# Seven block products in two more places and at half depth: a fused two-block network, 512 tokens, one core

## The reference

```python
# first block
mix = sigmoid(g_a) * (fox @ w_fox_up) + sigmoid(g_b) * (nsa @ w_nsa_up)
x = x + mix @ w_out                       # then the expert layer
# second block
proj = rmsnorm(h, g_pre) @ w_in           # gate_logits are its last 2 x 1024 columns
y_a = rwkv7_branch(...)                   # recurrence in chunks of 32 tokens, then @ w_out_a (512 x 1024)
y_b = mla_branch(...)                     # attention, then @ w_out_b (512 x 1024)
g_a, g_b = sigmoid(gate_logits + b_gate)
h = h + rmsnorm((g_a * y_a + g_b * y_b) @ w_o, g_post)
```

## Time and profile before

| | us |
|---|---|
| three runs | 1466.65, 1468.12, 1472.21 |
| median | 1468.12 |
| profiled execution, its time | 1459.77 |
| its span, first to last instruction | 1458.5 |
| PE busy | 1386.6 |
| DVE, ACT, POOL busy | 551.8, 347.0, 272.2 |

### The profile page before, as it was taken

The page is one execution under the profiler, slowest core; times in us unless marked ns, Lnnn a source line. Parts: engine busy times, 40 slices in busy tenths (PEclk is TensorE's granted clock), DMA queues, the critical chain, the costliest instruction groups (busy, mean ns, idle before and its releaser), DMA issues. The chain is left out here.

```text
span 1458.5 us, 24128 instructions
## 1 busy us (share of the span) xinstructions
PE 1386.6 (95%) x10276; PEld 786.6 (54%) x10276; DVE 551.8 (38%) x1338; ACT 347.0 (24%) x827; POOL 272.2 (19%) x311
## 2 busy tenths in 40 slices
PE   7998999899999997999999999999999899999997
PEld 4545544667858445444444434456877445556543
DVE  3124423574111625512211133444359581333403
ACT  2124324543101001111111123444221201322221
POOL 3010302203311641022222122010231002111000
PEclk9899999999999998999999999999999999999999
DMA  6154013220131267799999991010140421300211
GB/s 205 58 200 182 1 58 89 81 96 4 59 115 58 71 246 292 265 372 363 371 380 379 388 340 65 21 58 2 57 173 29 116 87 38 124 3 17 101 73 58
DMA packets 98975, 207.79 MB, mean 142 GB/s; under 512 B 14534, under 2 KB 22545, under 8 KB 98737
## 3 DMA queue, kind: packets, MB, share of 16 engines
q1 hardware_dynamic: 87152, 171.38, 32.7%
q0 software_dynamic: 11712, 34.83, 7.1%
HBM read 185.73 MB, written 19.42 MB: 141 GB/s over the span
## 5 line engine op out<-in xcount | busy, mean ns | idle before, releaser
L471 PE MATMUL pb<-Wt,HT 128*128 128x512 f32 (+1 forms) x384 | 154.7, 562 | 0.5 <-DMA Wt<-in_w_in_dram 0.5
L3620 PE MATMUL pb<-Wt,HT 128*128 128x512 f32 x256 | 117.8, 602 | 2.3 <-DVE AR L3711 2.3
L471 PEld LDWEIGHTS pb<-Wt,HT 128*128 128x128 f32 x384 | 71.4, 207 | 71.0 <-issue 71.0
L2183 PE MATMUL pb<-AR 128*64 128x512 f32 x256 | 85.0, 595 | 0.7 <-issue 0.7
L3620 PEld LDWEIGHTS pb<-Wt,HT 128*128 128x128 f32 x256 | 46.4, 190 | 54.1 <-issue 49.2
L683 PE MATMUL pb<-AR 64*128 64x512 f32 (+7 forms) x256 | 63.6, 494 | 11.1 <-ACT AR L778 4.5
L2183 PE MATMUL pb<-Wt,AR 128*64 128x512 f32 x192 | 70.8, 595 | 0.0
L782 ACT ACTIVATE AR<-AR,SM 128x512 f32<-128x512 f32 (+3 forms) x96 | 53.1, 554 | 51.6 <-DVE SM L734 51.2
L734 DVE CUSTOM_DVE_ANT_0 AR<-pb,AR 128x512 f32<-128x512 f32 (+3 forms) x96 | 43.2, 488 | 57.6 <-PE pb L685 57.4
L1547 PE MATMUL pb<-HT,Wt 128*128 128x256 f32 x288 | 65.0, 380 | 0.0
L3632 PE MATMUL pb<-Wt,AR 128*128 128x512 f32 x128 | 59.9, 605 | 0.9 <-ACT AR L810 0.8
(11 more groups left out here) (569 smaller groups left out, 2411.3 us busy)
## 6 DMA issues: line engine op xcount, KB each, us to landing
Wt<-in_w_in_dram SPq DMA_DIRECT2D x18, 2048.0 KB, 8.1
AR<-in_w_gate_dram SPq DMA_DIRECT2D x8, 2048.0 KB, 18.7
AR<-in_w_up_dram SPq DMA_DIRECT2D x8, 2048.0 KB, 18.7
AR<-in_w_down_dram SPq DMA_DIRECT2D x8, 2048.0 KB, 17.8
Wt<-in_w_gate_dram SPq DMA_DIRECT2D x6, 2048.0 KB, 18.2
Wt<-in_w_down_dram SPq DMA_DIRECT2D x6, 2048.0 KB, 14.2
Wt<-in_w_up_dram SPq DMA_DIRECT2D x6, 2048.0 KB, 21.1
ys<-AR POOLq DMA_DIRECT2D x1, 6144.0 KB, 22.5
```

Source lines behind the costliest of these rows:

```text
L471: r = mm(s[:, 0:n], lT[:, k, t * 128:(t + 1) * 128], w[:, k, c0:c0 + n], start=k == 0, stop=k == nk - 1)
L2183: r = mm(s[o:o + 64, :], XT[b % 2][:, k, 0:64], W.ap((n, b))[:, k, :], start=k == 0, stop=k == 7)
L3620: r = mm(s, HT[:, k, t * 128:(t + 1) * 128], W.ap(("gate2", c, br))[:, k, :], start=k == 0, stop=k == 7)
```

## The change

1. *First merge.* The up projections become `Quarters` units too, of half the depth (`self.h` is 2 instead of 4, so a product has 8 instructions of 256 columns). The order is gate, gate, up, up for each branch; a unit's product 4 comes behind the next unit's product 1. VectorE multiplies the results into the gates as they come and, in the last unit, mixes rows 0 to 3 between. GpSimd gets the left sums of both attention outputs.
2. *Output projection of the first block.* The first right sum moves into the last merge unit, the other sums alternate with the left ones, and the additions of product 1 into X are split: two early, four at the end.
3. *Branch b's gate* becomes two more `Quarters` units (u, v) with channels as rows, bias and sigmoid on ScalarE with a bias column (a new small load at the start), in 28 dense steps; its up projections follow with channels as rows, in 16 steps. Their right sums go behind those of z_a on GpSimd, the group norm's and bias loads and the decayed keys come behind them. The values' turns use rings T and O.
4. *Mixed rows of branch a* are turned tile by tile, at the start of the next tile's gates, and added out of PSUM by VectorE.
5. *Last projection* by `Seven` (`fin7`): 56 instead of 64 matmul pairs, both halves of w_o at its start, GpSimd's sums beside it, and a new order of the last rows.
6. All of GpSimd's sums of blocks are cut into pieces of 512 elements (`tiles_po`).
7. SP loads both gates' weights ahead of both up weights.

```diff
+        def tiles_po(out, a, b, op, sem):
+            n, w = out.shape[1], out.shape[2]
+            s = max(1, 512 // w)
+            for k in range(0, n, s):
+                r = gt.tensor_tensor(out[:, k:k + s, :], a[:, k:k + s, :], b[:, k:k + s, :], op)
+            r.then_inc(sem, 1)
...
+            def right_po(self, between=None):
                 t1, t2, t4 = self.rights
                 b = self.before
-                po.wait_ge(*W.loaded(self.tag))
+                po.wait_ge(*W.loaded(self.name))
                 if b is not None:
                     po.wait_ge(*b.part(1))
-                gt.tensor_tensor(t1, self.b12, self.b11, ALU.subtract).then_inc(self.right_sem, 1)
+                tiles_po(t1, self.b12, self.b11, ALU.subtract, self.right_sem)
                 if b is not None:
                     po.wait_ge(*b.part(2))
                 po.wait_ge(*self.right(1))
-                gt.tensor_tensor(t2, self.b22, t1, ALU.subtract).then_inc(self.right_sem, 1)
-                gt.tensor_tensor(self.b12, self.b22, self.b12, ALU.subtract).then_inc(self.right_sem, 1)
+                tiles_po(t2, self.b22, t1, ALU.subtract, self.right_sem)
+                tiles_po(self.b12, self.b22, self.b12, ALU.subtract, self.right_sem)
...
             def product(self, bank, s, t, go_on=False):
                 for i in range(2):
                     o, q = bank[:, 256 * i:256 * i + 256], slice(128 * i, 128 * i + 128)
-                    for k in range(4):
+                    for k in range(self.h):
                         lhs, rhs = (s[:, k, q], t[:, k, :]) if self.by_rows else (t[:, k, q], s[:, k, :])
-                        m = mm(o, lhs, rhs, start=i == k == 0 and not go_on, stop=k == 3, skip_group_check=True)
+                        m = mm(o, lhs, rhs, start=i == k == 0 and not go_on, stop=k == self.h - 1, skip_group_check=True)
...
+        merge7 = []
         for b, to in enumerate((mix, sg1)):
-            for c in range(2):
-                gates7.append(Quarters(("gate", c, b), 2 * b + c, merge_use, to[:, 4 * c:4 * c + 4, :], False,
-                                       gates7[-1] if gates7 else None))
+            for kind, use in (("gate", gate_use), ("up", up_use[b])):
+                for c in range(2):
+                    tag = ("gate", c, b) if kind == "gate" else ("up", b, c)
...
+            for n, u in enumerate(merge7):
+                u.right_po((lambda: out7.right_po(1)) if n == 7 else None)
+                if n == 0:
+                    left_sums_po(foT, 2, up_sums, s_uleft[0])
+                if n == 4:
+                    po.wait_ge(*P.filled(merge7[3].key("y")))
...
+            for n, u in enumerate(merge7):
+                if n == 2:
+                    pe.wait_ge(s_loc, 1)
+                u.p1_pe()
+                if n:
+                    merge7[n - 1].p4_pe()
+                u.p5_pe()
+                u.p2_pe()
+                u.p6_pe()
+                u.p3_pe()
+                u.p7_pe()
+            u.p4_pe()
 
...
+                    last = b == c == 1
+                    u.p5_ve()
+                    ve.wait_ge(*P.drained(g.key("x")))
+                    ve.wait_ge(*P.filled(u.key("x")))
+                    vt.tensor_tensor(u.c11, u.view("x"), u.c11, ALU.mult).then_inc(P.free(u.key("x")), 1)
+                    u.p6_ve()
+                    if last:
+                        mix_ve(0)
+                    ve.wait_ge(s_sg, 3 * (2 * b + c + 1))
...
         def ffn_norm_po():
-            out7.right_po()
             po.wait_ge(s_mix, 8)
-            out7.left_po(mixT)
+            out7.left_po(mixT, 1)
+            out7.right_po(2)
+            out7.left_po(mixT, 2)
             for i in range(2):
                 po.wait_ge(*out7.first(i))
-                for s in (X[:, i, 512:1024], X[:, 2 + i, 512:1024], X[:, 2 + i, 0:512]):
-                    gt.tensor_tensor(s, s, firsts[i], ALU.add).then_inc(s_fadd, 1)
+                gt.tensor_tensor(X[:, 2 + i, 512:1024], X[:, 2 + i, 512:1024], firsts[i], ALU.add).then_inc(s_fadd, 1)
+            out7.left_po(mixT, 3)
+            out7.right_po(3)
+            out7.left_po(mixT, 4)
+            for t, c in ((0, 512), (1, 512), (2, 0), (3, 0)):
+                gt.tensor_tensor(X[:, t, c:c + 512], X[:, t, c:c + 512], firsts[t % 2], ALU.add).then_inc(s_fadd, 1)
...
+        mx = Place(AR, ARN, tail_at).take(8, 512)
+        gate_use = dict(feature_use, rights=weight_sums[0:2] + [Place(flat_dif, 1024).take(4, 256)])
+        gates_b = []
+        for c in range(2):
+            gates_b.append(Quarters(("gate2", c, 1), len(merge7) + len(units), gate_use, mx[:, 4 * c:4 * c + 4, :], False,
+                                    units[-1]))
+            units.append(gates_b[c])
+        def dif_free_po():
...
-                s = P.take(pe, "S", ("vt", n))
+                s = P.take(pe, "TTOO"[n], ("vt", n))
...
+        def gates_b_pe():
+            u, v = gates_b
+            for f in (u.p1_pe, u.p5_pe, u.p2_pe, u.p6_pe, u.p3_pe, u.p7_pe, v.p1_pe, u.p4_pe, v.p5_pe, v.p2_pe, v.p6_pe,
+                      v.p3_pe, v.p7_pe, v.p4_pe):
+                f()
+                yield 1
+                yield 1
+        def ups_b_pe():
+            pe.wait_ge(s_ob, 4)
+            for m in range(8):
+                c, q = m // 4, slice(128 * (m % 4), 128 * (m % 4) + 128)
+                pe.wait_ge(*W.loaded(("up2", c, 1)))
+                s = P.take(pe, "O", ("ub", m))
+                for k in range(4):
+                    r = mm(s, W.ap(("up2", c, 1))[:, k, q], oBT[:, k, :], start=k == 0, stop=k == 3)
...
+        def mixed_turn_pe(c, t, ring):
+            pe.wait_ge(*P.drained(("u2", 0, c, t)))
+            turn4_pe(("mxt", c, t), sgr[c], 4, ring)
+        def mixed_add_ve(c, t):
+            key, o = ("mxt", c, t), mx[:, 4 * c:4 * c + 4, t * 128:(t + 1) * 128]
+            ve.wait_ge(*P.filled(key))
+            vt.tensor_tensor(o, P.ap(key).rearrange("p (m q) -> p m q", q=128), o, ALU.add).then_inc(P.free(key), 1)
...
+            yield from gates_b_pe()
+            yield from ups_b_pe()
+            for t in ALLT:
+                if t > 0:
+                    mixed_turn_pe(0, t - 1, "O")
                 for c in range(2):
-                    yield from gate_pe(0, c, t)
+                    for i, _ in enumerate(gate_pe(c, t)):
+                        if t > 0 and c == i == 0:
+                            mixed_turn_pe(1, t - 1, "O")
+                        yield 1
                 while t not in ended:
                     yield 1
-                if t == 3:
-                    for u in range(3):
-                        for c in range(2):
-                            mixed_turn_pe(c, u)
-                        yield 1
                 pe.wait_ge(s_out2, t + 1)
                 turn4_pe(("oAt", t), oA[:, t, :], 4, "O")
...
+                if n == 2:
+                    u.p5_ve()
+                if n == 4:
+                    u.p6_ve()
+                if n == 5:
+                    u.c12_ve()
+                if n == 6:
+                    u.c22_ve()
+                if n == 8:
+                    u.c21_ve()
+                if n == 9:
+                    v.p5_ve()
+                if n == 11:
+                    v.p6_ve()
+                if n == 12:
+                    v.c12_ve()
+                if n == 13:
+                    v.c22_ve()
+                if n == 14:
+                    v.c21_ve()
+                if n > 14:
+                    up(n - 15)
...
+            w = fin7.steps_pe(mxT, ready)
+            next(w)
+            for d in range(2):
+                mixed_turn_pe(d, 3, "T")
+            for _ in w:
+                pass
...
+            first_rows(0)
+            with_third(0)
+            first_rows(1)
+            with_third(1)
+            high_gain(0)
+            high_gain(1)
+            with_last(0)
+            low_gain(0)
+            root(2)
+            with_last(1)
+            last_rows(0)
+            low_gain(1)
+            root(3)
+            last_rows(1)
...
-            po.wait_ge(s_yc, 8)
             gt.dma_start(X[:, :, :], xv).then_inc(s_fin, 16)
+            po.wait_ge(s_out2, 4)
+            po.wait_ge(*P.filled(("oAt", 3)))
+            fin7.right_po(1)
+            for c in range(2):
+                po.wait_ge(*P.drained(("g2", 0, c, 3)))
+                for t in ALLT:
+                    po.wait_ge(*P.drained(("mxt", c, t)))
+            fin7.left_po(mxT, 1)
+            fin7.right_po(2)
+            fin7.left_po(mxT, 2)
+            fin7.left_po(mxT, 3)
+            fin7.right_po(3)
+            fin7.left_po(mxT, 4)
...
                 load(name, wcols(w2, c0, 512))
             for c in range(2):
                 load(("gate2", c, 1), wcols(w2, 3104 + 1024 + 512 * c, 512))
+            for c in range(2):
                 load(("up2", c, 1), wcols(a["w_out_b_2"], 512 * c, 512, 512))
                 if c == 0:
                     inverse_sy()
```

(53 more changed lines are left out.)

491 lines of the change are left out of this document (272 added, 219 removed).

## The result

The changed kernel takes 1494.01 us (median of 4 runs, 1490.24 to 1496.34) against 1468.49 us beside it (4 runs, 1466.65 to 1472.21): ratio 1.017, interval 1.014 to 1.020. That is 25.5 us slower, where 10.3 us faster was forecast. The profiled execution took 1492.46 us, its span is 1491.1 us.

The account below looks back on a forecast made before the run. TensorE, busy 95% of the span, was taken as the bound. Terms of -4.6 (merge), -0.1 (second branch's gate) and -5.6 (last projection) sum to -10.3 us, giving 1457.8 us, range 1449 to 1470.

Parts of the forecast that it names:

- A, first merge: First block's merge and output projection: products save 6.5 us, new waits cost 1.9, net -4.6 us (bounds -6.5 and +1).
- R3: Rival: merge's short units wait 1.5 us each, GpSimd's chain comes 2 late at the output projection; 1466 us, chance 0.13.
- B (1), contention: Last feature unit: each GpSimd piece takes 0.6 us from VectorE, so TensorE starts the block products 2.4 us later.
- R1: Rival: GpSimd's pieces cost VectorE their full 1.23 us, block products 7.7 us late; 1464.6 us, chance 0.18.
- B (2), inverse rows: Second block's weave: inverse rows precede gate additions on VectorE, TensorE waits 4.55 us against 2.31, +2.2 us.
- R2: Rival: VectorE's order in the inverse; above 3.45 us lag, 8 dependent products each wait a pair; 1475.7 us, chance 0.09.
- B (3), ring O: Second branch's gate: turns take one O bank, so gate tiles wait for the previous addition; +1.0 us (0 to 4).
- B (4), end of the weave: Last tile: fewer dense steps and a gate addition before the norm cost 1.5 us, one turn wait goes; net +0.8 us.
- wrong if TensorE waits over 12 us more than before in the weave: Sign against the forecast, second block's weave: over 12 us more TensorE waiting than before would prove it wrong.
- C, last projection: Last projection: two fewer products' worth of work saves 6.9 us, a longer tail costs 1.3; net -5.6 us (bounds -7 and -2).

Follow-up runs that it names:

- (4): Changed kernel with the eight right sums of the second branch's two gate units cut to 4 columns of one tile each; 1478.69 us, ratio 1.012.
- (6): Kernel (5) with 3 instead of 1 idle chunk steps ahead of the block products and 1 instead of 2 behind the first chunk group; 1472.24 us.
- (5): Kernel (1) with GpSimd making the first second-branch gate unit's second to fourth right sums only after the last decays are applied; 1457.91 us, ratio 0.993.
- (11): Kernel (5) unchanged, measured and profiled again, the best kernel of the study; 1457.33 us, ratio 0.991.
- (8): Kernel (5) with the first block's merge as in the kernel before, GpSimd's reordered chain for the output projection kept; 1460.92 us, ratio 0.996.
- (3): Changed kernel with GpSimd's sums whole, no longer cut into pieces of 512 elements; 1493.57 us, ratio 1.022.
- (1): Changed kernel with 2 instead of 5 idle chunk steps behind the first chunk group; 1459.65 us, ratio 0.998.

## Why the prediction was wrong, step by step

**A, first merge: the mechanism right, 0.9 us too much.** 3.7 instead of 4.6 us at the output projection. The waits at product 2 came twice, 0.19 us each, and the last product 4 waited 1.18 for an addition. GpSimd's reordered chain held: from the output projection's start to the last turns of the next norm it is 55.0 and 55.1 us. R3 did not happen.

**B (1), contention: the price of a piece a little low, what follows from it too low by half.** The prediction said 0.6 a piece, VectorE's rows give 0.71. It then let VectorE's idle 1.5 us absorb a part, for 2.4 in all; 5.1 us were lost. (The 5.7 us that (4) gave back are 0.57 for each of 10 pieces, but that is luck: 1.8 of them are half clock of TensorE.) The addition that product 4 of the last feature unit waits for was 2.5 us late instead of 0.9, TensorE waited 3.39 us, and the half clock that followed cost 1.8 more. R1 gave 7.7.

**B (2), inverse rows: forecast 4.55 us, measured 2.9** (2.02 and 0.88 at the two products 4; nothing at product 2) against 2.31 in the earlier trace rows: +0.6 instead of +2.2. R2 did not happen: in (6) one product's lag did exceed its limit of 3.45 (4.32 us), but the other product 4 waited 0.9, and no chain of waits followed.

**B (3), ring O: 1.0 forecast.** The waits of gates for an addition sum to 1.1 us.

**B (4), end of the weave: the step that failed.** It said that the dense side has 44 + 53 steps for 48 + 55, and then asked only what the last tile does: normed row ready at 1378.2, TensorE there at 1377.7, 0.8 us net. The same 4 steps stand ahead of all four turns. The sum for tile 0 was there to be made from the trace of the kernel before, 9.27 us of work between less 2.35 of slack; the prediction took group norm's readiness for one tile out of four. The last tile itself waited 1.11, near the 0.8. The four waits together cost 15.8 us where 0.8 stood, and the stretches at half clock, some 11.5 us behind these and the other waits, were in no term. The stop of 4.19 us was in none either. The line "wrong if TensorE waits over 12 us more than before in the weave" named the case (it was 23.0), with no chance of its own.

**C, last projection: right.** 5.6 us forecast, 5.6 in the traces. The start waited 1.68 us for the second weight half, which the prediction had ready 1.2 us ahead (in the best kernel it doesn't wait); the tail is 8.8 us for 9.1 forecast.

**Sum.** Forecast -4.6, -0.1, -5.6. By the traces -3.7 for the merge, +5.1 and +27.8 for the second branch's gate, -5.6 for the last projection, and +1.8 of scatter ahead of the merge: +25.4 without the pause, against 25.5 by the medians. With the distance restored and the sums moved, the whole change is worth 9.5 us (5) and 10.8 us (11) by the medians, 0.7 to 0.9%: about the 10.3 us that were forecast are there, behind waits that the change itself had made. That the sum fits so well is in part luck, for (5) and (11) are not the kernel that it was made for.

## What to carry to other kernels

Where two lists of work are dealt into one program at a fixed ratio, shortening one moves every meeting point of the two. Work out at each meeting, not at the last one alone, what work stands between and how much slack it leaves, and adjust the idle steps of the other list in the same edit. Give a long wait of TensorE a second price for the half clock behind it: here 15.8 us of such waits, with the others of the stretch, cost some 11.5 more by subtraction. And place GpSimd's sums where VectorE is not the bound, even if TensorE needs them only little later.

## What the runs showed of the hardware

- The waits of 3.2 to 7.8 us that TensorE had in the second block's weave and last feature unit were followed by a stretch at half clock (64 z products of 1.95 us took 3.40 behind 6.91 us, a product of 3.6 took 5.38 behind 3.39), and the single ones of 2.4 us (5) and 2.0 us (changed kernel, product 4) by none: 3.69 us there. The length alone does not decide it: 2.72 us at that product in (8) was followed by 5.38 us, 3.16 us in the merge of (3) by 3.69, and two waits of 2.38 and 2.03 us within 5 us, at the block products of (1), by a clock of 0.52 from 1152 to 1160.
- A GpSimd sum and a VectorE operation with both operands in SBUF hold up each other: the scan of 1.22 us takes 2.29, a pair of pieces of 2.50 takes up to 4.37. A copy of 16 columns, 0.17 us alone, took 1.06 there. Pieces of 512 elements cost 4.7 us less in this stretch than whole sums of 1024.
- ScalarE stood still for some 8 us beyond its operands while GpSimd issued gathers, in 8 of the 13 profiles, of kernels with and without the change; in these the stretch from merge to features is 6 to 8 us longer. Why is open.
- TensorE stood still for 4.2 to 4.5 us within a row of equal matmuls while 2 MB of weights landed, at the same matmul of the changed kernel, (3) and (4); in the other kernels at most 1.8 us in that row. Why is open.
